# A hybrid RG-LRU and attention layer: the fourth gate group moved up behind the third, into another accumulator

## The reference

```python
rx, rgx, qx, kx, vx, gax, gbx = split_cols(hx @ w_in[l])          # 1024 latent tokens
rc, rgc, qc, kc, vc, gac, gbc = split_cols(hc @ w_in[l])          # 256 context tokens
# recurrence, for each of two directions, on xc = dwconv(r, conv_w, conv_b)
r = sigmoid(einsum('blnc,ncd->blnd', xg, w_a) + b_a)              # 16 blocks of 64 channels
i = sigmoid(einsum('blnc,ncd->blnd', xg, w_x) + b_x)
log_a = -LRU_C * r * softplus(-lam)
a = exp(log_a)
b = sqrt(-expm1(2.0 * log_a)) * (i * xc)
h = linear_scan(a, b, h0)
y_rx = (hf + hb) * gelu(rgx)
y = sigmoid(gax) * (y_rx @ w_o_rnn) + sigmoid(gbx) * (y_ax @ w_o_attn)
```

## Time and profile before

| | before |
|---|---|
| median of 3 runs | 1771.83 us (1771.51 to 1772.38) |
| the profiled execution's own time | 1773.39 us |
| its span, first to last instruction | 1771.6 us |
| PE busy | 1733.3 us, 98% of the span |
| DVE busy | 1209.3 us, 68% |
| ACT busy | 775.6 us, 44% |
| POOL busy | 537.2 us, 30% |
| mean granted TensorE clock | 0.997 |

### The profile page before, as it was taken

The page is one execution under the profiler, slowest core; times in us unless marked ns, Lnnn a source line. Parts: engine busy times, 40 slices in busy tenths (PEclk is TensorE's granted clock), DMA queues, the critical chain, the costliest instruction groups (busy, mean ns, idle before and its releaser), DMA issues.

```text
span 1771.6 us, 23341 instructions
## 1 busy us (share of the span) xinstructions
PE 1733.3 (98%) x8382; PEld 1436.3 (81%) x8382; DVE 1209.3 (68%) x1386; ACT 775.6 (44%) x1016; POOL 537.2 (30%) x262
## 2 busy tenths in 40 slices
PE   7998999999999999989999999999999999999998
PEld 5887788887788889878888877888888888888887
DVE  7977666778406587877246389999999898424425
ACT  5348778888101188840011145444444444202205
POOL 1035666665345576635457700000000000000000
PEclk9999999999999999999999999999999999999999
DMA  9231111111454300047226412221221224523112
GB/s 373 73 108 32 63 57 51 50 50 54 142 179 120 83 25 0 1 166 262 77 75 236 132 60 96 83 95 71 83 94 71 83 89 161 202 100 132 54 36 95
DMA packets 56149, 177.98 MB, mean 100 GB/s; under 512 B 11794, under 2 KB 12178, under 8 KB 55444
## 3 DMA queue, kind: packets, MB, share of 16 engines
q1 hardware_dynamic: 46964, 148.27, 23.7%
q10 hardware_dynamic: 9120, 28.84, 4.9%
HBM read 140.39 MB, written 31.46 MB: 97 GB/s over the span
## 4 chain that ended last, share of the span: by engine, by line
PE 79%; DVE 7%; ACT 2%; issue 2%; DMA 1%; POOL 1%; SPq 0%; ACTq 0%; DVEq 0%; POOLq 0%
PE acc L919 17%; PE acc L921 17%; PE acc L920 17%; PE gp L919 8%; PE gp L921 8%; PE gp L920 8%; PE gp L1065 2%; PE acc L1225 1%; DMA wst<-in_w_in 1%; DVE y_lo L2335 1%; DVE T_lo L2636 0%; PE gp L1200 0%; PE gp L1199 0%; PE gp L1198 0%; DVE prob L2384 0%
## 5 line engine op out<-in xcount | busy, mean ns | idle before, releaser
L919 PE MATMUL acc<-hx_hi,whi_both 128*128 128x512 f32 x672 | 265.5, 395 | 3.7 <-ACT sg L1458 1.6
L920 PE MATMUL acc<-hx_lo,whi_both 128*128 128x512 f32 x672 | 262.8, 391 | 0.0
L921 PE MATMUL acc<-hx_hi,wlo_both 128*128 128x512 f32 x672 | 262.3, 390 | 0.0
L731 POOL TENSOR_TENSOR whi_both<-wst,ones 128x1024 fp32r<-128x1024 f32 x56 | 149.5, 2670 | 256.4 <-PE acc L921 242.5
L733 POOL TENSOR_TENSOR wlo_both<-wst,whi_both 128x1024 fp32r<-128x1024 f32 x56 | 172.0, 3071 | 4.4
L919 PEld LDWEIGHTS acc<-hx_hi,whi_both 128*128 128x128 f32 x672 | 126.8, 189 | 36.4 <-issue 5.0
L921 PEld LDWEIGHTS acc<-hx_hi,wlo_both 128*128 128x128 f32 x672 | 126.7, 189 | 26.8
L920 PEld LDWEIGHTS acc<-hx_lo,whi_both 128*128 128x128 f32 x672 | 126.8, 189 | 25.3
L1458 ACT ACTIVATE dn_hi<-wst 128x768 fp32r<-128x768 f32 x32 | 26.9, 843 | 182.5 <-PE acc L921 121.0
L919 PE MATMUL acc<-T_hi,fac_hi 128*128 128x512 f32 x264 | 102.8, 389 | 0.4 <-DVE fac_lo L2675 0.4
L920 PE MATMUL acc<-T_lo,fac_hi 128*128 128x512 f32 x264 | 102.7, 389 | 0.0
(11 more groups left out here) (394 smaller groups left out, 4632.9 us busy)
## 6 DMA issues: line engine op xcount, KB each, us to landing
wst<-in_w_in SPq DMA_DIRECT2D x43, 512.0 KB, 3.5
wst<-in_w_up SPq DMA_DIRECT2D x26, 512.0 KB, 4.1
wg<-in_mod_rest ACTq DMA_DIRECT2D x24, 512.0 KB, 5.3
ffn_row_scratch<-ca SPq DMA_DIRECT2D x24, 512.0 KB, 2.6
wst<-in_w_down SPq DMA_DIRECT2D x32, 384.0 KB, 3.1
g_in<-ffn_row_scratch SPq DMA_DIRECT2D x24, 512.0 KB, 7.1
wup<-in_w_up SPq DMA_DIRECT2D x22, 512.0 KB, 4.0
wmod<-in_mod_first SPq DMA_DIRECT2D x16, 512.0 KB, 15.4
```

Source lines behind the costliest of these rows:

```text
L731: nc.gpsimd.tensor_tensor(whi[s][:, 0:kc, :], wst[s][:, 0:kc, :], ones_of(kc), mult).then_inc(S["w_hi"], 1)
L919: mm(out_ap, w_h, x_h, start=first, stop=False)
L920: mm(out_ap, w_h, x_l, start=False, stop=False)
L921: return mm(out_ap, w_l, x_h, start=False, stop=last)
```

## The change

The fourth gate group (q = 3) of chunks 1 to 6 is computed into `acc[0]`, the accumulator of the gelu row, in place of `gp`. On TensorE it stands right behind the third; both halves of the merge gate row stand behind it, with nothing between them. It no longer waits for the reading of the third group, but for the gelu of its own chunk (`acc_read[0]`). The gelu row of the step, which overwrites `acc[0]`, now also waits for `gate_read` of all four groups. ScalarE reads group 3 ahead of the first merge half. Chunks 0 and 7 keep their order and their banks.

```diff
--- before.py
+++ after.py
@@ -366,6 +366,11 @@
             return W_S1 - 4 + 3 * e + part
 
         gate_bank = gp[:, 3 * HALF:4 * HALF]
+        def gate_out(c, q):
+
+            of_last = q == 3 and not (isinstance(c, int) and c in (0, KC - 1))
+            return acc[0] if of_last else gp
+
         gate_parts = ((0, 0, HALF), (0, HALF, ALL), (1, HALF, ALL), (1, 0, HALF))
 
         first_out = (gp[:, 0:SEQ], gp[:, SEQ:2 * SEQ], acc[1][:, :], acc[0][:, :])
@@ -1051,8 +1056,11 @@
                 if q == 0:
                     pe.wait_ge(S["g_ready"], c + 1)
                     pe.wait_ge(S["xc_lo"], c + 1)
-                if not (isinstance(c, int) and c == 0 and q == 0):
+                if gate_out(c, q) is not gp:
+                    slot_read(pe, A_S1 + 1, 2, c)
+                elif not (isinstance(c, int) and c == 0 and q == 0):
                     pe.wait_ge(S["gate_read"], 4 * c + q)
+                bank = gate_out(c, q)
                 d, first, end = gate_parts[q]
                 wide = HALF if end - first == HALF else CTX
                 for c0 in range(first, end, wide):
@@ -1062,7 +1070,7 @@
                             rows, o = slice(64 * b, 64 * b + 64), (end - first) * b + c0 - first
                             if (t, b, c0 - first) == (0, 0, HALF):
                                 pe.wait_ge(S["gate_first"], 2 * c + q)
-                            last = mm(gp[:, o:o + wide], w[rows, d, :], x[rows, x0:x0 + wide], start=t == 0, stop=t == 2)
+                            last = mm(bank[:, o:o + wide], w[rows, d, :], x[rows, x0:x0 + wide], start=t == 0, stop=t == 2)
                             if (t, b, c0 - first) == (2, 1, 0) and wide == CTX:
                                 last.then_inc(S["gate_first"], 1)
                 last.then_inc(S["gate_full"], 1)
@@ -1114,13 +1122,14 @@
                 gate(i - 1, 1)
                 half(A_S1, n_r, 1, hx_hi, hx_lo).then_inc(S["acc_full"], 1)
                 gate(i - 1, 2)
+                gate(i - 1, 3)
                 weights(n_ga, 6, j)
                 pe.wait_ge(S["rc_read"], i + 1)
                 merge_gate_half(i, n_ga, 0)
-                gate(i - 1, 3)
                 merge_gate_half(i, n_ga, 1)
                 weights(n_rg, 6, j)
                 slot_free(A_S1 + 1, 2, i)
+                pe.wait_ge(S["gate_read"], 4 * i)
                 half(A_S1 + 1, n_rg, 0, hx_hi, hx_lo)
                 half(A_S1 + 1, n_rg, 1, hx_hi, hx_lo).then_inc(S["acc_full"], 1)
 
@@ -1614,11 +1623,12 @@
                     act.wait_ge(S["m_done"], 2 * c - 1 + d)
                     act.wait_ge(S["b_done"], 2 * c - 1 + d)
                 act.sem_inc(S["passed_act"], 1)
+                bank = gate_out(c, q)
                 for b in range(2):
                     bias = colat(pcol, (C_GAB, C_GXB)[b] + KC * d, c)
                     for t, dst in enumerate((sr[d], si[d])):
                         rows, o = slice(64 * t, 64 * t + 64), (end - first) * b
-                        last = act_of(dst[64 * b:64 * b + 64, first:end], gp[rows, o:o + end - first], ACT.Sigmoid, bias=bias[rows, :])
+                        last = act_of(dst[64 * b:64 * b + 64, first:end], bank[rows, o:o + end - first], ACT.Sigmoid, bias=bias[rows, :])
                 last.then_inc(S["gate_read"], 1)
 
             def decays(c):
@@ -1672,9 +1682,9 @@
                     act.wait_ge(S["ksv_stored"], 16 * 4)
                     gate_sigmoid(0, 2)
                     centre(1, e)
+                gate_sigmoid(i - 1, 3)
                 if later(i, 2):
                     merge_gate_half(i, 0)
-                gate_sigmoid(i - 1, 3)
                 decays(i - 1)
                 roots(i - 1)
                 gelu(i)
```

## The result

| | before | changed |
|---|---|---|
| median, first comparison | 1772.41 us (1770.99 to 1774.87, 8 runs) | 1778.38 us (1775.65 to 1779.66, 8 runs) |
| median, second comparison | 1772.18 us (1770.89 to 1773.69, 28 runs) | 1777.07 us (1776.02 to 1778.35, 8 runs) |

The changed kernel is slower by a factor of 1.0030 (95% interval 1.0021 to 1.0039) in the first and 1.0029 (1.0018 to 1.0039) in the second comparison, 6.0 and 4.9 us. The two intervals overlap, so the 1.1 us between them is not a difference that was shown. Forecast were +3.0 us and no measurable change, with a range that ended at 1777.0.

What follows compares the result with a forecast made beforehand. TensorE's list was taken as the bound (busy 1733.3 of 1771.6 us). Pauses in steps 2 to 6 +4.1, step 7 -0.6, clock -0.5: +3.0, 1774.8 us, no measurable change; range 1772.2 to 1777.0.

Steps and rivals of the forecast that it cites:

- TensorE alone would gain 0.40: Joining group 3 to group 2 saves a tiling-mode entry and exit: 0.40 us in each of six steps, 2.4 us.
- The step is 0.77 longer: Second merge half waits for `sgh`: +0.77 us a step, 0.86 in the loop; bounds 0.58 and 1.04; steps 2-6 +4.1.
- What it gives back behind step 7: The gelu's table load hides behind the gelu row, so the wait of `gate(7, 1)` shrinks to 0.2 us: -0.6 us.
- What the clock adds: With a shorter wait for chunk 7, the half-clock stretch behind it stays away: 0 to -1.7 us, taken as -0.5.
- Within 0.2% ... can't tell from no change: Differences within 0.2% (3.5 us) were taken as unmeasurable, so the forecast was no measurable change, close to the edge.
- What costs nothing: Group 3's wait for its chunk's gelu, the gelu row's for `gate_read`, and `split_conv` running earlier delay nothing.
- A: Rival: slower by the pauses' length; loop steps cost the upper bound 1.04 us, +4.2, 1776.1 us; chance 0.32.
- B: Rival: slower by the clock; each new 0.9 us pause may halve it, costing up to 1.7 us, 1776.5; chance 0.10.

Runs made afterwards that it cites:

- e3: The changed kernel with the second merge half in a bank of its own (third bank of `gp`); 1770.18 us, ratio 0.9988 to the kernel before.
- e5: The changed kernel with ScalarE's old order, the first merge half's sigmoid ahead of group 3's; 1776.6 us, ratio 1.0023 to the kernel before.
- e1: The changed kernel with ScalarE's steps 4 to 7 written out instead of looped; 1775.23 us, ratio 1.0018 to the kernel before.
- e2: The kernel before with ScalarE's steps 4 to 7 written out, nothing else; 1771.82 us, ratio 0.9999 to the kernel before.
- e7: The changed kernel with the second merge half in its own bank and ScalarE's steps 4 to 7 written out; 1768.75 us, ratio 0.9982 to the kernel before.
- e4: The kernel before with group 3 of chunks 1 to 6 in `acc[0]` and its new waits, old order kept; 1772.17 us, ratio 1.0000.
- e10: The changed kernel unaltered, timed again in the second batch; 1777.07 us, ratio 1.0029 to the kernel before.
- e6: The changed kernel with VectorE's work held until POOL's products of chunk 7 are done; 1776.74 us, ratio 1.0025 to the kernel before.

## Why the prediction was wrong, point by point

- **"TensorE alone would gain 0.40"** held: 0.40 to 0.43 us a step in e3. Six times that is 2.4 to 2.6; the median moved by 2.0, which the interval (0.5 to 3.7 us) allows. The Trainium skill, page "TensorEngine Tiling (Array Packing)", section Key Properties, says that a change of the tiling mode drains the engine. e3 fits that, with 0.40 to 0.43 us for one entry and exit less; that a drain is what costs them, no run here shows.
- **"The step is 0.77 longer"** in steps 2 and 3, and 0.86 in the loop, held to 0.01, so the +4.1 for steps 2 to 6 is right (measured +4.1): the interval of a step is 25.15 in steps 2 and 3 of the changed kernel and 25.22 to 25.23 in steps 4 to 7, against 24.37, so +0.78 and +0.85 to 0.86. In step 7 the second half starts 8.68 us behind group 2 (388.85 - 380.17); 7.83 + 0.86 = 8.69 was worked out. The split was right too: by the bank alone the bound was 0.58, and e5 has 0.55 and 0.56 in the two written-out steps.
- **"What it gives back behind step 7"** (-0.6) is the step that failed, in the sentence "The load has no wait on it in the order of instructions, so it hides behind the row". That was read from step 3, which is written out, and used for step 7, which is in the loop. There the wait stands ahead of the load, on the instruction that computes the gelu's place in `Y`. The earlier trace rows could not show it: in the kernel before the row ended at 400.23 (399.84 + 0.39) and the sqrts at 400.41, so the wait was over when ScalarE came to it. The change made TensorE 0.85 us later and ScalarE's `decays` earlier, and so turned a wait that cost nothing into one that puts the 1.28 us of the load on the path. The term was -0.6; the trace has +0.75: step 7 is 0.85 longer, and the wait behind it only 0.10 shorter. e1 lets the load run ahead and gets 1.37 us back, the size of the error; e2 shows that the same edit is worth nothing in the kernel before. By the Trainium skill, page "ScalarE: Activation LUTs", section What ACT_TABLE_LOAD costs, the load on the path would cost 1.28 us and a drain of 1.38; e1 against the changed kernel has 1.37 for both together, and the runs decide.
- **"What the clock adds"**, -0.5, did not come. It rested on the wait falling to 0.2 us, and the wait stayed at 1.46 us. The clock behind it was 1.00 all the same. Of the eight profiles with a wait of 1.21 to 1.56 us there, two have the slow stretch behind it, the one of before and that of e5; with one profile of the kernel before, how many of its timed runs had it stays unknown. The two terms together, -1.1 forecast and +0.75 measured, are the 1.9 us between +3.0 and +4.9.
- **"Within 0.2% ... can't tell from no change"** was too wide for these comparisons: their intervals reach 0.1% to either side, and the 2.0 us of e3 and the 3.4 us of e7 were told from none. The stated range also misses by 0.1 us the lower bound that it was to take in (1772.1 against 1772.2).
- **"What costs nothing"** held. e4 shows it for the accumulator and its waits. `split_conv` did meet POOL and took 3.24 us where it took 0.83, and nobody waited:

```profile
219.26 3.24 DVE L2264 CAST xch<-xc 128x1280 fp32r<-128x1280 f32 x1
222.54 3.57 DVE L2266 TENSOR_TENSOR xcl<-xc,xch 128x1280 fp32r<-128x1280 f32 x1
```

The sum with the term put right is 2 x 0.78 + 4 x 0.86 - 0.10 = +4.9 us. From `gate(1, 1)`'s long wait to `gate(7, 1)` the traces say the same: 249.49 us (163.99 to 413.48) against 244.62 (163.72 to 408.34), +4.87. The second comparison measured +4.9; that they agree so closely is partly luck, since the executions of one kernel lie 1 to 5 us apart. The first has 1.1 more, which its interval allows; the wait for POOL adds 1.4 us (2.04 - 0.62) to an execution that has it, its profiled one did, but how many of the eight had it was not recorded, so this share stays open. The two profiled executions differ by 5.0 us (1778.43 - 1773.39): +0.3 ahead of step 2's long wait (163.99 - 163.72), +4.9 to `gate(7, 1)`, -1.6 for the clock behind it (to the next gate group 6.93 us against 8.53), +1.4 for POOL, and 0.1 that was not traced.

Of the rivals, A (1776.1) and B (from 1776.5) had the outcome right, slower, but not the mechanism. A's pauses did not cost the upper bound. B did not happen: the pauses of 0.9 us were followed by no fall of the clock.

## What to carry to other kernels

Before moving work from between two writers of one bank, ask what covered the read between them; if nothing does afterwards, the second writer needs a bank of its own (here the difference between +4.9 and -2.0 us). Look up where a wait stands in the very step that the argument speaks of: a looped step and a written-out one of the same code can hold it on different sides of a table load, and here did where the activation's output lay at a place that the loop computes. And a wait that costs nothing in the trace of before can be the next bound; compare how much later each side may come before it does.

## What the runs showed of the hardware

**The slow stretches of the clock differ from execution to execution of one program.** Behind the same 3.8 us wait at 164 us (the clock is given as a share of full speed), the granted clock was 0.72 over 6 us in the changed kernel's first profile and 0.62 over 9 us in e10, the same program:

```profile
162.00:168.00 6.00, 4.01 (x24) 3.46 (x25) 5.93 (x4) 3.47 (x5) 0.00 (x0) 0.72 0.00 0
```

```profile
162.00:171.00 9.00, 7.33 (x32) 6.06 (x33) 7.50 (x7) 5.74 (x8) 0.00 (x0) 0.62 0.00 0
```

That is 1.7 us (6 x 0.28) against 3.4 us (9 x 0.38) of full clock withheld. From the end of the wait to gate group 2, TensorE takes 8.38 us in the one and 9.75 in the other. On one chip it is the same: e6 and e10, whose programs differ only 270 us later, take 8.46 and 9.75 us there. Behind `gate(7, 1)`, a 1.56 us wait had 0.57 and 1.46 us waits had 1.00 in both profiles of the changed kernel; in e5, behind 1.55 us, the stretch from 414 to 420 has 0.72, and in e4, behind 1.56 us, it is 1.00. One profile doesn't tell what the clock costs a kernel, and a difference of 1.3 to 1.6 us between two profiles needs no cause in the program.

**Which of POOL and VectorE is slowed where they meet also differs** between two profiles of one program: 6.24 and 3.49 us in one, 2.82 and 8.46 in the other. Why it falls one way or the other, no run here tells; which chip the first was taken on is not recorded either. Of the nine profiles in which they meet (all but that of e6), VectorE was slowed in eight.
